# Attention queries and keys computed token-stationary, rotated there and turned by transfers, with the first weight blocks split in another order, in a two-layer hybrid trunk on one core

## The reference, cut to what matters

```python
qkv = (x @ w_qkv).reshape(bsz, seqlen, 3, ATTN_HEADS, ATTN_HEAD_DIM)   # 16 heads of 128
q = (_partial_rope(q, cos, sin) * (ATTN_HEAD_DIM ** -0.5)).transpose(0, 2, 1, 3)
k = _partial_rope(k, cos, sin).transpose(0, 2, 1, 3)
...
def _partial_rope(t, cos, sin):          # the first 32 of the 128 columns of a head
    t1, t2 = t32[..., :half], t32[..., half:ROPE_DIM]
    return jnp.concatenate([t1 * c - t2 * s, t2 * c + t1 * s, t32[..., ROPE_DIM:]], axis=-1)
...
p = jax.nn.softmax(s, axis=-1)           # causal; then p @ v, and o @ w_out
```

## Time and profile before

| | |
|---|---|
| median of 3 runs | 2098.49 us (2097.46 to 2098.7) |
| the profiled execution's own time | 2096.86 us |
| its span in the trace | 2095.0 us |
| granted TensorE clock | 1.00 |
| PE busy | 2085.9 us (100%), 9918 matmuls |
| DVE busy | 1290.4 us (62%) |
| ACT busy | 975.1 us (47%) |
| DMA | 439.80 MB, mean 210 GB/s, 16 engines busy 66% |

### The profile page before, as it was taken

How to read it: one execution, slowest core, us unless ns; L and a number is a source line. 1 busy time by engine, 2 the same in 40 slices (tenths; PEclk the granted TensorE clock), 3 DMA queues, 4 the chain that set the end, 5 groups by cost and what they waited for, 6 DMA issues and landing times.

```text
span 2095.0 us, 28820 instructions
## 1 busy us (share of the span) xinstructions
PE 2085.9 (100%) x9918; PEld 1749.5 (84%) x9918; DVE 1290.4 (62%) x1246; ACT 975.1 (47%) x1172; POOL 21.3 (1%) x16
## 2 busy tenths in 40 slices
PE   9999999999999999999999999999999999999999
PEld 8898888888888888888988888888888888888887
DVE  6869666665555565555766667675665554555565
ACT  5596455434444443443644445454434443443442
POOL 0000010000000000000000000010000000000000
PEclk9999999999999999999999999999999999999999
DMA  7665758766766766775654556658666766766763
GB/s 257 195 197 189 235 180 261 250 200 203 236 222 183 238 230 201 219 233 171 193 186 158 168 167 225 202 189 267 216 210 212 241 206 195 243 218 228 241 212 120
DMA packets 233547, 439.80 MB, mean 210 GB/s; under 512 B 15056, under 2 KB 37840, under 8 KB 232432
## 3 DMA queue, kind: packets, MB, share of 16 engines
q1 hardware_dynamic: 232032, 432.79, 65.2%
q10 hardware_dynamic: 1424, 5.77, 0.7%
HBM read 419.63 MB, written 18.87 MB: 209 GB/s over the span
## 4 chain that ended last, share of the span: by engine, by line
PE 99%; DMA 0%; ACT 0%; issue 0%; DVE 0%; ACTq 0%
PE ps L427 75%; PE ps L419 11%; PE ps L416 5%; PE ps L726 1%; PE ps L725 1%; PE ps L724 1%; PE ps L558 1%; PE ps L739 0%; DMA wst<-in_rg_w_in_dram 0%; PE ps L524 0%; PE ps L523 0%; PE ps L525 0%; PE ps L596 0%; PE ps L714 0%; PE ps L599 0%; PE ps L575 0%
## 5 line engine op out<-in xcount | busy, mean ns | idle before, releaser
L1014 DVE TENSOR_TENSOR wl<-wst,wh 128x1024 fp32r<-128x1024 f32 x743 | 887.8, 1219 | 327.3 <-ACT wh L757 324.0
L757 ACT ACTIVATE wh<-wst 128x1024 fp32r<-128x1024 f32 x743 | 769.8, 1059 | 649.1 <-PE ps L427 411.8
L427 PE MATMUL ps<-wh,hid 128*128 128x512 f32 x2560 | 695.9, 390 | 0.0
L427 PEld LDWEIGHTS ps<-wh,hid 128*128 128x128 f32 x2560 | 479.5, 188 | 98.9
L427 PE MATMUL ps<-wh,xin 128*128 128x512 f32 x2048 | 548.9, 389 | 0.0
L427 PEld LDWEIGHTS ps<-wh,xin 128*128 128x128 f32 x2048 | 383.9, 188 | 79.4
L427 PE MATMUL ps<-wl,hid 128*128 128x512 f32 x1280 | 404.6, 389 | 0.0
L419 PE MATMUL ps<-xin,wh 128*128 128x512 f32 x960 | 331.2, 395 | 0.8 <-DVE wl L1014 0.8
L427 PE MATMUL ps<-wl,xin 128*128 128x512 f32 x1024 | 315.2, 389 | 0.0
L427 PEld LDWEIGHTS ps<-wl,hid 128*128 128x128 f32 x1280 | 240.2, 188 | 50.0
L416 PE MATMUL ps<-xin,wl 128*128 128x256 f32 x960 | 256.8, 278 | 0.0
(11 more groups left out here) (138 smaller groups left out, 835.9 us busy)
## 6 DMA issues: line engine op xcount, KB each, us to landing
wst<-in_mlp_w_dram SPq DMA_DIRECT2D x512, 512.0 KB, 4.7
wst<-in_moba_w_qkv_dram SPq DMA_DIRECT2D x96, 512.0 KB, 4.6
wst<-in_rg_w_in_dram SPq DMA_DIRECT2D x62, 512.0 KB, 4.1
wst<-in_rg_w_out_dram SPq DMA_DIRECT2D x32, 512.0 KB, 4.9
sq_by_quad<-f SPq DMA_DIRECT2D x128, 128.0 KB, 2.5
f<-sq_by_quad SPq DMA_DIRECT2D x32, 512.0 KB, 5.1
wst<-in_moba_w_out_dram SPq DMA_DIRECT2D x32, 512.0 KB, 5.3
f<-in_x_dram SPq DMA_DIRECT2D x8, 256.0 KB, 6.3
```

Source lines behind the costliest of these rows:

```text
L427: return pe.matmul(banks(half)[:, a, :], src[:, c, part, a * P:(a + 1) * P], (wl if low else wh)[:, s, w], start=(c == 0 and part + low == 0),
L757: act.activation(wh[:, off % SPLITS, :], wst[:, slot, :], ACT.Copy).then_inc(wh_done, 1)
L1014: dve.tensor_tensor(wl[:, off % SPLITS, :], wst[:, off % STAGE, :], wh[:, off % SPLITS, :], ALU.subtract).then_inc(wl_done, 1)
```

## The change

Queries and keys use the token form, so all three turns of a group have one form. Their PSUM results alternate between banks 0/1 and 2/3; scores are in banks 4 to 7, probabilities times v in 6 and 7. ACT evicts a result by partition quarters into `qk_out`; quarter 0 holds the 32 rotated columns of each head, and DVE rotates it there (`rotate`). Sixteen transfers of 32 partitions x 1 KB, SBUF to SBUF, eight issued by SP and eight by ACT, exchange the quarters (twelve as soon as the eviction is done, four after the rotation), and DVE turns 32x32 pieces (`turn_qk`). The probabilities go the same way with 16 transfers of 32 partitions x 1.5 KB (`move_p`, `turn_p`), in place of PE's transposes and ACT's copies. Scores stand before the last block of the v turn, and the product with v behind the first block of the next group's k turn (of the last group: inside the output projection, whose first two turns are interleaved as in the MLP, so that the rows of group 3 are used late). The loops over groups are written out.

At the beginning ACT and DVE split the weights of block 0 (first half) and of blocks 2 and up ahead of the x rows, and block 1 comes and is split in halves (the first issued by ACT, the second by SP).

```diff
+        def part_moves(dst, src, of, to=range(GROUP)):
+            return [(dst[q * 32:(q + 1) * 32, i, :], src[i * 32:(i + 1) * 32, q, :]) for q in to for i in of]
...
@@ SP
+            def move_qk(g, part):
+                sp.wait_ge(qk_evict, HALVES * (2 * g + part + 1))
+                if 2 * g + part:
+                    sp.wait_ge(qk_ready, 2 * g + part)
+                for dst, src in part_moves(qk_quad, qk_out, (0, 1), range(1, GROUP)):
+                    sp.dma_start(dst, src).then_inc(qk_moved, 16)
+                sp.wait_ge(qk_rotated, 2 * g + part + 1)
+                for dst, src in part_moves(qk_quad, qk_out, (0, 1), (0,)):
+                    sp.dma_start(dst, src).then_inc(qk_moved, 16)
...
+            for g in range(NG):
+                k_before = {2: lambda: move_qk(g - 1, 1)} if g else {}
+                p_before = {3: lambda: move_p(g - 1)} if g else {}
+                for part, also in enumerate((k_before, p_before, {2: lambda: move_qk(g, 0)})):
+                    load_turn(moba_w_qkv[0], part * D + g * COLS, B_QKV + (3 * g + part) * BLOCKS, also)
...
@@ PE
+            for g in range(NG):
+                b = B_QKV + 3 * g * BLOCKS
+                own, other = 2 * (g % 2), 2 * (1 - g % 2)
+                if g == 0:
+                    begun_token_turn(1, b, R_LN1)
+                else:
+                    pe.wait_ge(qk_evict, HALVES * 2 * g)
+                    token_turn(xin, own, b, R_LN1)
+                    pe.wait_ge(v_stored, g)
+                token_turn(xin, other, b + BLOCKS, R_LN1, {1: lambda: weighted(g - 1)} if g else {})
+                pe.wait_ge(qk_evict, HALVES * (2 * g + 1))
+                token_turn(xin, own, b + 2 * BLOCKS, R_LN1, {BLOCKS - 1: lambda: scores(g)})
-                    pe.wait_ge(p_ready, g + 1)
-                    for h in range(GROUP):
-                        for k in range(3):
-                            mm = pe.transpose(Y[:, h, k * P:(k + 1) * P], prob[:, h, k * P:(k + 1) * P],
-                                              ident[:, :])
-                        mm.then_inc(pt_done, 1)
...
@@ ACT
+            def take_qk(g, part, first):
+                act.wait_ge(mm_done, B_QKV + (3 * g + part + 1) * BLOCKS)
...
+                for a in range(HALVES):
+                    by_part = qk_out.rearrange("p q (c a r) -> p a c q r", c=GROUP, a=HALVES)[:, a]
+                    by_col = ps[:, first + a, :].rearrange("p (c q r) -> p c q r", c=GROUP, q=GROUP)
+                    act.activation(by_part, by_col, ACT.Copy).then_inc(qk_evict, 1)
...
+                for dst, src in part_moves(qk_quad, qk_out, (2, 3), range(1, GROUP)):
+                    act.dma_start(dst, src).then_inc(qk_moved, 16)
+                act.wait_ge(qk_rotated, 2 * g + part + 1)
...
@@ DVE
+            def turn_qk(g, part, dst):
+                dve.wait_ge(qk_moved, MOVES * (2 * g + part + 1))
+                dve.transpose(dst.rearrange("p c (a i t) -> p i (c a) t", a=HALVES, t=32),
+                              qk_quad.rearrange("p i (b r) -> p i b r", r=32)).then_inc(qk_ready, 1)
+            for g in range(NG):
+                b = B_QKV + 3 * g * BLOCKS
+                splits(b, START, START + 2)
+                if g:
+                    turn_p(g - 1)
+                splits(b, START + 2, LATE + 1)
+                rotate(g, 0)
+                splits(b, LATE + 1, NEXT)
+                b += BLOCKS
+                splits(b, START, START + 2)
+                if g:
+                    weighted_lo(g - 1)
+                turn_qk(g, 0, qg)
...
@@ the beginning, on ACT (on DVE in the same order)
+            for k, q, landed in ((0, 0, first_half[0]), (0, 1, stage_full[0]), (1, 0, first_half[1])):
+                act.dma_start(wst[:, k, q * COLS:(q + 1) * COLS], first[k, :, q, :]).then_inc(landed, 16)
...
             for k in range(BLOCKS):
+                if k == 0:
+                    split_half_hi(k, 0, first_half[k], first_hi[k])
+                elif k > 1:
+                    split_hi(0, 0, k)
                 act.wait_ge(xt_done, k + 1)
                 act.activation(xin[:, k * KCH:(k + 1) * KCH, 0, :], xt_bank(k), ACT.Copy).then_inc(xt_hi, 1)
+                if k == 1:
+                    split_half_hi(k, 0, first_half[k], first_hi[k])
+                if k < 2:
+                    split_half_hi(k, 1, stage_full[k], wh_done)
```

More of the change, by code:

```diff
@@ L438, in token_turn @@
                             for a in range(HALVES):
-                                mm = token_step(src, half, a, c, part, low)
+                                mm = token_step(src, first, a, c, part, low)
                     mm.then_inc(mm_done, 1)
@@ L617, in begun_token_turn, with scores, weighted @@
                     mm.then_inc(mm_done, 1)
+            def scores(g):
+                S = banks(1)
+                pe.wait_ge(qk_ready, 2 * g + 2)
+                if g:
+                    pe.wait_ge(pair_ready, R_ATT + 2 * g)
+                for h in range(GROUP):
+                    pe.matmul(S[:, h, 0:P], qg[:, h, 0:P], kg[:, h, 0:P], start=True, stop=True)
+                    mm = pe.matmul(S[:, h, P:3 * P], qg[:, h, P:T], kg[:, h, :], start=True, stop=True)
+                mm.then_inc(scores_done, 1)
+            def weighted(g):
+                pe.wait_ge(pt_ready, g + 1)
+                pe.wait_ge(v_stored, g + 1)
+                for h in range(GROUP):
+                    o_ap = ps[:, 6 + h // 2, (h % 2) * T:(h % 2 + 1) * T]
+                    pe.matmul(o_ap, vg[:, 0, h * P:(h + 1) * P], probt[:, h, 0:2 * P], start=True, stop=False)
+                    mm = pe.matmul(o_ap[:, P:T], vg[:, 1, h * P:(h + 1) * P], probt[:, h, 2 * P:3 * P],
+                                   start=False, stop=True)
+                mm.then_inc(pv_done, 1)
             def output_sums(free):
@@ L924, in out_unit @@
             def out_unit(b0, n):
-                act.activation(tok[:, 1, 0:1], eps[:, 0:1], ACT.Sqrt)
-                for j in range(2):
-                    splits(b0 + j * BLOCKS, b0 // BLOCKS + j, START, NEXT)
+                if n == 0:
+                    act.activation(tok[:, 1, 0:1], eps[:, 0:1], ACT.Sqrt)
+                    splits(b0, b0 // BLOCKS, START, NEXT)
+                else:
+                    splits(b0, b0 // BLOCKS, START, LATE + 2)
+                    weighted_hi(NG - 1)
+                    act.activation(tok[:, 1, 0:1], eps[:, 0:1], ACT.Sqrt)
+                    splits(b0, b0 // BLOCKS, LATE + 2, NEXT)
+                splits(b0 + BLOCKS, b0 // BLOCKS + 1, START, NEXT)
                 last_pair(b0 + 2 * BLOCKS, b0 // BLOCKS + 2, n)
@@ new lines, in exponentials, with move_p @@
+            def exponentials(g):
+                act.wait_ge(bias_ready, g + 1)
+                for h in range(GROUP):
+                    for a, cols in enumerate((slice(0, P), slice(P, 3 * P))):
+                        ex = act.activation(prob[:, h, cols], prob[:, h, cols], ACT.Exp, scale=QK_SCALE,
+                                            bias=stat[:, h, 2 + a:3 + a], accum_out=stat[:, h, 4 + a:5 + a])
+                ex.then_inc(exp_done, 1)
+            def move_p(g):
+                act.wait_ge(p_ready, g + 1)
+                for dst, src in part_moves(prob_quad, prob_out, (2, 3)):
+                    act.dma_start(dst, src).then_inc(p_moved, 16)
@@ new lines, in _, with rotate @@
+            dve.wait_ge(prm_loaded, 16 * 8)
+            def rotate(g, part):
+                n = 2 * g + part
+                dve.wait_ge(qk_evict, HALVES * (n + 1))
+                if n:
+                    dve.wait_ge(qk_rotated, n)
+                dve.tensor_tensor(cosd, turned, cos_t, ALU.mult)
+                for lo, other in ((0, ROPE_HALF), (ROPE_HALF, 0)):
+                    half, swapped = slice(lo, lo + ROPE_HALF), slice(other, other + ROPE_HALF)
+                    ins = dve.tensor_tensor(rot[:, :, :, half], turned[:, :, :, swapped], sin_t[:, :, :, half],
+                                            ALU.mult)
+                ins.then_inc(qk_link, 1)
+                dve.wait_ge(qk_link, n + 1)
+                dve.tensor_tensor(turned, cosd, rot, ALU.add).then_inc(qk_rotated, 1)
```

388 lines of the change are left out of this document (180 added, 208 removed).

## The result

| | before | after |
|---|---|---|
| median | 2098.59 us (2097.46 to 2098.74, 4 runs) | 2084.35 us (2083.68 to 2085.62, 4 runs) |
| ratio, 95% interval | | 0.9934 [0.9917, 0.9951] |
| profiled execution, its span | 2096.86, 2095.0 us | 2084.47, 2082.7 us |
| PE matmuls | 9918 | 9566 |
| DVE, ACT busy | 1290.4, 975.1 us | 1268.0, 969.6 us |

The change is faster by 14.2 us in the medians; the forecast was a gain of 11.4, a time of 2087.1 and a range from 2085.0. The direction and the mechanism hold, the size is 2.8 us too small, and the time lies 0.65 us under the range.

The account below looks back on a forecast made before the run. PE's own list was taken to bound the kernel. Terms of 7.0, 2.2, 0.2, 1.2 and 0.8 us made a gain of 11.4 us off the median of 2098.49, giving 2087.1 us, range 2085.0 to 2091.5.

Parts of the forecast that it names:

- Bound, and nothing waits: Whole kernel: PE's own list sets the time, and PE should not wait in attention at all.
- The three rivals that had PE waiting for moves or weights: Attention: small waits at joints (2091.1 us, 10%), moves one after another (2119.9, 4%), weights starving (2099, 3%).
- Transposes, 7.0 us: PE in attention: transposes of probabilities and the wait behind them go, 1.75 us in each of four groups.
- Form of q and k, 2.2 us: Groups 1 to 3: token form gains 0.93 us a group, less a restart of 0.20, leaving 0.73 × 3.
- a restart of 0.20: Product with v inside the k turn: PE's restart charged at the 0.20 us seen behind the scores, bound 0.
- Group 0, 0.19 + 1.22 us: Group 0's early-begun q turn: gain 0.19 us to the turn's rest, 1.22 us from there to the v turn.
- The beginning, 0.8 us, bounds 0 and 1.0: Program start: PE's 0.8 us wait for block 1's low half goes; 0 if it reappears at block 2.
- The sum: Whole kernel: 7.0 + 2.2 + 0.2 + 1.2 + 0.8 = 11.4 us gain, taken off profiled execution and median.
- The range: Whole kernel: 2085.0 to 2091.5 us, from the terms' bounds, a run spread of 1.2 us and the small waits.
- The chains: Work beside PE in attention stays hidden: cover 7 to 9 us for probabilities, 8 to 10 us for keys.
- The page on issue gaps: Rival that the form brings nothing, from 518 and 262 cycles for 512 and 256 columns: 2091.3 us, 2%.
- that rival: Moves in attention go one after another, loss 64x − 127 us: 2119.9 us at x = 2.5, 4%.

Follow-up runs that it names:

- d2: The changed kernel with the q and k turns of groups 1 to 3 back in the column form: 2087.18 us, ratio 0.9955.
- d1: The kernel before without each group's 12 transposes of probabilities and ACT's copies of them, product still behind the v turn: 2096.62 us, ratio 1.0.
- f1: The kernel before, unchanged, a single further profile on a fourth chip: span 2096.8 us, time 2098.57 us.
- f2: The kernel before, unchanged, one more single profile on the fourth chip: span 2096.8 us, time 2098.66 us.
- c2: The kernel before, unchanged, run and profiled again: 2098.22 us (11 runs).
- c3: The kernel before with only the new beginning (order of first splits, block 1 in halves): 2097.13 us, ratio 0.9995.
- e2: The changed kernel with the product with v of groups 0 to 2 two blocks earlier, before the next q turn's last block: 2085.15 us.
- d4: The changed kernel with each of the 16 transfers of a move cut in two, same bytes: 2109.85 us, ratio 1.0064.

## Why the prediction fell short

- **Bound, and nothing waits.** Right. Rows 1 to 4 told it: PE's list sets the end, and every chain beside it stayed covered. The three rivals that had PE waiting for moves or weights did not occur.
- **Transposes, 7.0 us.** Right in size: of the 2.71 us of a group, 1.84 are left beside the 0.87 that `d2` gives the form. `d1` shows that they and the product's move are one term: without the move 1.6 of the 7.0 are there.
- **Form of q and k, 2.2 us.** This is the step that failed, a term of the sum that was sized too small, in two ways. The 0.93 a group came from a profile in which all q turns ran at the quick pace. At the slow pace, which `f1` and `f2` show in five turns of six, the form is worth 0.38 us more in each, up to 1.15 us in all, 4.0 in place of 2.2. And a restart of 0.20 was charged behind the product, which costs 0.09 there, no more than the old q turn paid behind its own product: the first two matmuls at 1078.00 in `c2` take 0.71 us, the two at 1100.28 take 0.62. The group's 2.71 us is 1.75 + 0.96, so the form term should have been 0.96 × 3 = 2.9. The prediction named the bound "0" for the restart and did not take it.
- **Group 0, 0.19 + 1.22 us.** Right: its rest starts 1008.61 − 1001.40 = 7.21 us behind the first early matmul, and the v turn 38.18 later (1046.79), forecast 7.21 and 38.19.
- **The beginning, 0.8 us, bounds 0 and 1.0.** It gives 1.0 in the first pair of profiles and 1.2 in the medians of `c3`, with an interval that holds 0. The term itself holds: the program's first turn takes 25.8 to 26.9 us in the six profiles with the old beginning and 25.3 to 25.8 in the eight with the new, 0.9 less in the mean, and PE waits for the low half of a block in none of the eight (0 to 1.1 in the six). Not all of it stays. Between the fourth turn's start and the turn at 124.24 the eight take 0.6 us more in the mean; in seven of them PE waits there for ACT, by 0.3 to 1.4 us (L563 above), with the old beginning in two of six. That being early brings this wait is likely but not shown. And 0.4 of the first pair's 1.0 is the pace of the second column turn, slow before and quick after.
- **The sum.** By the first pair of profiled executions the gain is 2096.86 − 2084.47 = 12.4 us: 11.4 behind the milestone and 1.0 ahead of it. That is 1.0 above the forecast (0.7 from the form, 0.2 from the beginning). The other 1.8 up to 14.2 are the difference between this execution of before and its median; `f1` and `f2` put up to 1.15 of it in the pace of the q turns and the rest at the beginning. The execution, 2096.86 us, is quicker than all its timed runs (2097.46 to 2098.7), and the prediction took its gain off the median all the same. A profile of a quick execution shows the thing to be removed where it costs least.
- **The range.** It allowed 0.8 us more gain than the sum, from the bounds, and 1.2 for the spread of runs, but nothing for the 1.6 us between the profiled execution and the median. Carried as a bound of their own, they would have put the low end at 2083.4 and held 2084.35.
- **The chains.** Cover of the probabilities 4.9 us, not 7 to 9: v's eviction is now followed by a table load of 1.28 us ahead of the exponentials (before, ACT was idle for 4.92 us there, and such loads stand at 1018.62 and 1155.51, off this chain), issues take 0.6 us instead of 0.43 to 0.5, and the last piece landed later. It cost nothing here; `e2` shows that 5.4 us less would have.
- **The page on issue gaps.** By the gaps in the Trainium skill ("TensorE: Matmul & The Clock Gate", section "Back-to-back issue gap") the form would bring nothing. The section gives them for a single matmul, and some 131 ns for 512 columns in a stream. Here a token matmul takes 227 ns, so neither figure holds in this kernel; `d2` measures 2.6 us for six turns, and the trace's spacing decides.
- **The page on small transfers.** The Trainium skill ("DMA: Bandwidth & Descriptors", section "Rules for kernel authors") holds transfers under 64 KB to be mostly overhead. `d4` bears the warning out, though by another way than a fixed part paid in turn: the transfers overlap, and it is the issuing engine that pays, 0.6 to 0.7 us each. The prediction's own sum for that rival has a slip: at x = 2.1 the loss is 64 × 2.1 − 127 = 7.4 us and the gain left 4.0, not 5.

## What to carry to other kernels

- When the profiled execution is quicker than the median, ask which term of the sum could be larger in the others, and let the difference widen the range on the side of the gain; two or three profiles of the same kernel, compared matmul by matmul, show where executions differ. Look, too, whether the same form runs at another pace elsewhere in the profile at hand: here it did, in the first mixer.
- Work that is taken off a busy engine brings its full time only if what it covered has a new cover: here the transposes hid the eviction of v, and the product had to move as well.
- Count a transfer by its issue on the queue of an engine that has other work, and count what stands behind the issues on that engine and behind the loads on the others; the landing was seldom what ended a chain.

## What the runs showed of the hardware

- The column form (weights loaded, 512 and 256 tokens' columns streamed) has two paces, 22.19 to 22.28 us and 22.57 to 22.66 us for 128 matmuls, at the same granted clock and without a wait, in executions of the same kernel and within one execution. In attention only turns that follow the product with v showed the slower one, in the first mixer the turn behind other matmuls in all fourteen profiles and the second column turn in five. What brings it isn't settled.
- An SBUF to SBUF transfer of 32 partitions takes about 0.6 us to issue on SP and on ACT, alone or both at once (medians 0.59 and 0.61 to 0.62; 5.21 us for eight, 8.62 for twelve); in the profile of before the 128 KB transfers took 0.43.
- After PE waited for 8.17 us, the mean granted clock was 0.64 in the ten microseconds in which it began again, and three such waits of 21.6 us together came with a stretch longer by 28.0.
